# The first norm applied to the results of a projection, and its inputs loaded in pieces, in a one-core two-model kernel

## The reference

```python
def rmsnorm(x, g):
    xf = x.astype(jnp.float32)
    y = xf * lax.rsqrt(jnp.mean(xf * xf, axis=-1, keepdims=True) + EPS)
    return (y * g.astype(jnp.float32)).astype(x.dtype)

def retention_layer(h, g_norm, w_in, gn_gain, w_out):
    proj = rmsnorm(h, g_norm) @ w_in
    q, k, v, gate = jnp.split(proj, [RET_QK_W, 2 * RET_QK_W, 2 * RET_QK_W + RET_V_W], axis=-1)
    ...
    q = rotary(heads(q, RET_QK_DIM), pos)
    k = rotary(heads(k, RET_QK_DIM), pos) * (RET_QK_DIM ** -0.5)
    o = retention_chunkwise(q, k, heads(v, RET_V_DIM))
    mu = jnp.mean(o, axis=-1, keepdims=True)
    var = jnp.mean(jnp.square(o - mu), axis=-1, keepdims=True)
    o = ((o - mu) * lax.rsqrt(var + EPS)).transpose(0, 2, 1, 3).reshape(b, t, RET_V_W)
    o = o * gn_gain.astype(jnp.float32)
    y = (jax.nn.silu(gate.astype(jnp.float32)) * o).astype(h.dtype) @ w_out
    return h + y
```

## Time and profile before

| | us |
|---|---|
| median of 3 runs | 1091.26 |
| lowest and highest of them | 1089.37, 1096.87 |
| span of the profiled execution | 1088.2 |
| TensorE busy in it | 1037.3 (95%) |
| first product of unit 0 starts at | 16.92 |

### The profile page before, as it was taken

The page is one execution under the profiler, slowest core; times in us unless marked ns, Lnnn a source line. Parts: engine busy times, 40 slices in busy tenths (PEclk is TensorE's granted clock), DMA queues, the critical chain, the costliest instruction groups (busy, mean ns, idle before and its releaser), DMA issues.

```text
span 1088.2 us, 15874 instructions
## 1 busy us (share of the span) xinstructions
PE 1037.3 (95%) x6574; PEld 906.6 (83%) x6574; DVE 576.1 (53%) x708; ACT 468.7 (43%) x700; POOL 86.1 (8%) x88
## 2 busy tenths in 40 slices
PE   5999999998999999999999799997999889999996
PEld 5988778877989999977787599775788779999885
DVE  4864565456455546556535568556232455655543
ACT  5334454355554535455335545532223344444432
POOL 0000220000400001013100000002210000000000
PEclk9999999998999999999999899997798989999998
DMA  9545444543556643320254235330000235555551
GB/s 348 176 142 190 155 155 158 190 156 117 194 185 240 229 159 116 119 78 1 78 193 155 78 126 185 121 113 1 1 1 1 97 116 190 174 182 191 187 192 47
DMA packets 21555, 150.52 MB, mean 138 GB/s; under 512 B 2401, under 2 KB 2657, under 8 KB 3953
## 3 DMA queue, kind: packets, MB, share of 16 engines
q1 hardware_dynamic: 21488, 149.55, 39.5%
HBM read 148.49 MB, written 1.05 MB: 137 GB/s over the span
## 4 chain that ended last, share of the span: by engine, by line
PE 92%; DVE 3%; ACT 2%; DMA 1%; issue 1%; POOL 0%; SPq 0%; POOLq 0%; DVEq 0%
PE psum L657 90%; PE psum L991 1%; DMA ring<-in_weights 1%; ACT R L1311 1%; PE psum L731 0%; ACT xn L1311 0%; PE psum L1139 0%; ACT high_parts L1303 0%; ACT xT_parts L536 0%; PE psum L997 0%; DVE ring_parts L1631 0%; DVE h L1666 0%; ACT R L1595 0%; DVE xT_parts L546 0%; PE psum L1143 0%
## 5 line engine op out<-in xcount | busy, mean ns | idle before, releaser
L1631 DVE TENSOR_TENSOR ring_parts<-ring,high_parts 128x2048 fp32r<-128x2048 f32 x135 | 311.2, 2307 | 237.4 <-ACT high_parts L1303 236.7
L1303 ACT CAST high_parts<-ring 128x2048 fp32r<-128x2048 f32 x135 | 257.4, 1908 | 207.4 <-PE psum L657 179.1
L657 PE MATMUL psum<-xT_parts,high_parts 128*128 128x256 f32 (+1 forms) x1664 | 339.9, 283 | 1.3 <-DVE xT_parts L546 1.3
L657 PE MATMUL psum<-xT_parts,ring_parts 128*128 128x256 f32 (+1 forms) x1024 | 291.5, 285 | 0.0
L657 PEld LDWEIGHTS psum<-xT_parts,high_parts 128*128 128x128 f32 x1664 | 270.9, 189 | 1.7 <-DVE ring_parts L1631 1.5
L657 PEld LDWEIGHTS psum<-xT_parts,ring_parts 128*128 128x128 f32 x1024 | 192.8, 188 | 0.0
L657 PE MATMUL psum<-high_parts,xT_parts 128*128 128x512 f32 (+1 forms) x560 | 180.4, 399 | 1.6 <-DVE xT_parts L546 1.6
L657 PE MATMUL psum<-high_parts,R_parts 128*128 128x512 f32 (+1 forms) x560 | 167.3, 373 | 1.8 <-DVE R L2070 1.1
L657 PEld LDWEIGHTS psum<-high_parts,xT_parts 128*128 128x128 f32 (+1 forms) x560 | 103.9, 187 | 28.1 <-issue 3.2
L657 PE MATMUL psum<-ring_parts,xT_parts 128*128 128x512 f32 (+1 forms) x296 | 116.9, 395 | 0.0
L657 PEld LDWEIGHTS psum<-high_parts,R_parts 128*128 128x128 f32 (+1 forms) x560 | 99.2, 178 | 21.2 <-DVE R L2070 1.3
(11 more groups left out here) (249 smaller groups left out, 1082.7 us busy)
## 6 DMA issues: line engine op xcount, KB each, us to landing
ring<-in_weights SPq DMA_DIRECT2D x137, 1024.0 KB, 4.9
h<-in_x SPq DMA_DIRECT2D x2, 512.0 KB, 4.2
G<-in_gains SPq DMA_DIRECT2D x2, 512.0 KB, 11.8
out<-xn SPq DMA_DIRECT2D x2, 512.0 KB, 3.1
R<-in_ret_tabs SPq DMA_DIRECT2D x1, 768.0 KB, 10.1
tab<-in_tabs SPq DMA_DIRECT2D x1, 663.5 KB, 15.6
G<-in_p_t SPq DMA_DIRECT2D x1, 512.0 KB, 16.5
side_sb<-in_side SPq DMA_DIRECT2D x1, 512.0 KB, 17.2
```

The source lines that it names most:

```text
L657: return pe.matmul(out, lhsT, rhs, start=first, stop=last, skip_group_check=True)
L1303: act.copy(as_r(high[:, u % HIGH * UNIT:(u % HIGH + 1) * UNIT]), ring[:, u % RING * UNIT:(u % RING + 1) * UNIT]).then_inc(sem("units_high" ...
L1631: return dve.tensor_tensor(as_r(value), value, value_of(hi), ALU.subtract)
```

## The change

The norm of the first layer is no longer applied to `x`. TensorE turns `x` itself (`turn`), as soon as it and the identity are there. The roots come in later: spread over the partitions by two products (`spread_roots`, behind unit 2), multiplied into the rotation tables by VectorE (`token_rows`, `turned_by`), into the copies of v, into the scale of the gate's tanh (`half_rstd`) and into the roots of the group norm (`rooted`). `x` is loaded in four pieces of 128 x 512, unit 0 in four pieces of 128 x 512 issued by ScalarE's queue, and each piece is split by itself with semaphores of its own; the product of unit 0 goes piece by piece. Since unit 0 is not split by `split_units` any more, its count starts at 1.

```diff
         def split_units(engine, split, ahead):
-            done = [0]
+            done = [1]
...
-            for t in range(TT):
-                load(f"x_in{t}", hrow(t), x[t * P:(t + 1) * P, :])
+            def load_x(c):
+                for t in range(TT):
+                    load(f"x_in{t}{c}", hrow(t, c * 512, 512), x[t * P:(t + 1) * P, c * 512:(c + 1) * 512])
+
+            load_x(0)
             load("ident_in", ident, tabs[:, TB_ID:TB_ID + P])
             load("par_in", par[:, :], params)
+            load_x(1)
...
-            for u in range(2):
-                unit(u, weights[u])
+            unit(1, weights[1])
             load("ret_in", R[:, R4:R4 + NRT], ret_tabs)
...
+            def spread_roots(n):
+
+                pe.wait_ge(sem("roots"), ROOTS.index(("norm", n)) + 1)
+                bank = aux.open(pe, ("rows", n))
+                for t in range(TT):
+                    root = rstd[:, 2 * n + t:2 * n + t + 1].to_broadcast([P, P])
+                    ins = mm(bank[:, t * P:(t + 1) * P], root, ident, True, True)
+                aux.full(ins, ("rows", n), begun[0] - 2)
...
-            turn_norm("xT_ret", 0)
+            pe.wait_ge(sem("ident_in"), 16)
+            for f in range(4):
+                if f % 2 == 0:
+                    for t in range(TT):
+                        pe.wait_ge(sem(f"x_in{t}{f // 2}"), 16)
+                turn("xT_ret", f, h_tile)
             need("x", "xT_ret", 4)
-            for n in range(8):
+
+            bank = main.open(pe, ("rqk", 0))
+            w, product = next_unit(KD)
+            for f in range(4):
+                pe.wait_ge(sem(piece_low(f)), 1)
+                for half in range(2):
+                    for k in (2 * f, 2 * f + 1):
+                        ins = parts3(product, bank[:, half * T:(half + 1) * T], w(k, slice(half * P, (half + 1) * P)),
+                                     x_src(k, M, T), half == 0 and k == 0, k == KD - 1)
+            main.full(ins, ("rqk", 0))
+            for n in range(1, 8):
                 project_a([("rqk", n)], x_src, M, T)
+                if n == 2:
+                    spread_roots(0)
...
-            norm_stats(0, lambda c, t: act.wait_ge(sem(f"x_in{t}"), 16))
+            for f in range(4):
+                act.dma_start(ring[:, piece(f)], weights[0, :, piece(f)]).then_inc(sem(piece_in(f)), 16)
             act.wait_ge(sem("par_in"), 16)
+            for f in range(4):
+                high_parts("xT_ret", slice(f, f + 1))
+                act.wait_ge(sem(piece_in(f)), 16)
+                act.copy(as_r(high[:, piece(f)]), ring[:, piece(f)]).then_inc(sem(piece_high(f)), 1)
             split_up_to(1)
-            high_parts("xT_ret")
+            norm_stats(0, lambda c, t: act.wait_ge(sem(f"x_in{t}{c}"), 16))
             act.wait_ge(sem("meta_in"), 16)
...
+            act.wait_ge(sem("roots"), ROOTS.index(("norm", 0)) + 1)
...
-            dve.wait_ge(sem("ident_in"), 16)
-            norm(0)
             dve.wait_ge(sem("par_in"), 16)
+            for f in range(4):
+                low_parts("xT_ret", slice(f, f + 1))
+                dve.wait_ge(sem(piece_high(f)), 1)
+                low_part(high[:, piece(f)], ring[:, piece(f)]).then_inc(sem(piece_low(f)), 1)
...
             dve.wait_ge(sem("ret_in"), 16)
+            token_rows(0)
+            turned_by = R[:, R4 + RT_COS:R4 + RT_COS + 2 * T].rearrange("p (f t) -> p f t", f=2)
+            own.then_wait(dve.tensor_tensor(turned_by, turned_by, over(token_scale[:, M:TM], 2), ALU.mult))
...
+                rooted = rrs[:, four].rearrange("p (h t) -> p h t", t=TT)
+                own.then_wait(dve.tensor_tensor(rooted, rooted, over(rstd[:, 0:2], 2), ALU.mult))
```

More of the change, by code:

```diff
@@ L115 @@
 IS_SPLIT = [not name.startswith("ple_w_emb") for name, *_ in UNITS]
-SPLITS = [sum(IS_SPLIT[:u + 1]) for u in range(NU)]
+SPLITS = [sum(IS_SPLIT[1:u + 1]) for u in range(NU)]
 PARAM = {}
@@ L276, in aux_uses @@
 def aux_uses():
-    u = tr_uses("xT_ret", 0) + [("meta", "dve")]
+    u = tr_uses("xT_ret", 0) + [(("rows", 0), "dve"), ("meta", "dve")]
     u += [(("rs", h), "dve") for h in range(RH)]
@@ L427, in two_models_kernel @@
         power = cols(1)
+        half_rstd = cols(8)
         msum = cols(3)
@@ L525, in two_models_kernel @@
         turned("xT_ffn", range(4), (into_x, gain_of("ffn_norm_w_2")))
[L527 to L552, removed]
+        def turned_high(act, name, wait, some=slice(None)):
+            for key, parts, frees in [turn for turn in turns if turn[0][0] == name][some]:
+                bank = wait(aux, key)
+                if name == "xT_kv" and frees:
+                    act.wait_ge(sem("kv_low"), key[1] + 1)
+                for n, (kt, (hi, _), g) in enumerate(parts):
+                    ins = act.activation(as_r(hi), bank[:, n * T:(n + 1) * T], ACT.Copy, scale=g)
+                ins.then_inc(sem("turned_high"), 1)
@@ new lines, in turned_low @@
+        def turned_low(dve, name, wait, some=slice(None)):
+            for n_turn, (key, parts, frees) in [(n, turn) for n, turn in enumerate(turns) if turn[0][0] == name][some]:
+                bank = wait(aux, key)
+                dve.wait_ge(sem("turned_high"), n_turn + 1)
+                for n, (kt, (hi, lo), g) in enumerate(parts):
+                    ins = dve.scalar_tensor_tensor(as_r(lo), bank[:, n * T:(n + 1) * T], g, value_of(hi),
+                                                   ALU.mult,
+                                                   ALU.subtract)
+                if frees:
+                    aux.free(ins, key)
+                else:
+                    ins.then_inc(sem("kv_low"), 1)
@@ L1320, in norm_stats, with high_parts, gate_tanh @@
                         square(n, c, t, h, trash)
-            def high_parts(name):
-                turned_high(act, name, wait)
+            def high_parts(name, some=slice(None)):
+                turned_high(act, name, wait, some)
             gates = [0]
-            def gate_tanh(key, before):
+            def gate_tanh(key, before, scale=0.5):
                 i = gates[0]
@@ L1348, in _ @@
                     bank = wait(main, key)
-                    main.free(act.copy(R[:, R2 + t * 2048 + c * 512:R2 + t * 2048 + (c + 1) * 512], bank), key)
+                    main.free(act.activation(R[:, R2 + t * 2048 + c * 512:R2 + t * 2048 + (c + 1) * 512], bank, ACT.Copy,
+                                             scale=rstd[:, t:t + 1]), key)
             act.wait_ge(sem("rotated"), 8)
@@ L1639, in _, with low_parts @@
             wait, after_read, split_up_to = split_units(dve, split_low, HIGH - 1)
-            def low_parts(name):
-                turned_low(dve, name, wait)
+            def low_parts(name, some=slice(None)):
+                turned_low(dve, name, wait, some)
             def roots(n):
@@ L1660, in norm, with token_rows @@
                 to_diagonal(n)
+            def token_rows(n):
+                bank = wait(aux, ("rows", n))
+                aux.free(dve.tensor_copy(token_scale[:, M:TM], bank[:, 0:T]), ("rows", n))
+                after_read(aux, ("rows", n))
             def add_to_h(keys):
```

43 lines of the change are left out of this document (33 added, 10 removed).

## The result

| | before | after |
|---|---|---|
| median of 20 runs each, us | 1096.7 | 1103.89 |
| lowest and highest, us | 1088.77, 1101.53 | 1098.63, 1110.4 |
| span of the profiled execution, us | 1088.2 | 1108.6 |

What follows compares the result with a forecast made beforehand. TensorE, busy 95% of the span, was taken to bound the kernel. Start and clock in unit 0 3.65, roots' products 0.45 and wait at unit 4 2.1 sum to 6.2 us slower: 1091.26 to 1097.5, range 1092 to 1101.5.

Steps and rivals of the forecast that it cites:

- unit 1 lands: Opening: unit 1's transfer lands at 11.75 us as before, since the same bytes stand ahead of it.
- first product: Start of unit 0 on TensorE: at about 18.75 us instead of 16.92, behind unit 1's cast, table load and VectorE's pieces.
- lower clock in unit 0: Unit 0: TensorE, idle before, runs its first 4.0 us at the lower clock; the unit takes 7.5 us, not 5.68.
- roots' products: Behind unit 2: two added float32 products of 128 columns on TensorE cost +0.45 us.
- wait for units 2, 3: Units 2 and 3: their rests, later behind the meta tokens, stay hidden behind TensorE's work; term 0.
- wait at unit 4: Start of unit 4: TensorE waits for VectorE's copy, multiplication, two rotations and rest of unit 4; +2.1 us.
- units 4 to 7 behind it: After the wait at unit 4: VectorE's later work hides and units take 5.68 us each as before; no term.
- unit 1 lands earlier: Rival, opening: unit 1 lands about 2.4 us earlier since its queue no longer carries unit 0; +3.8 us in all, chance 0.06.
- the rival of the upper clock: Rival, unit 0: TensorE already at the upper clock, +4.2 us in all; chance 0.16, shared with a free table load.
- the clock's fall behind it: Rival, unit 4: the new wait lowers the clock for 4 us, costing 1.9; +8.1 us in all, chance 0.14.
- The change does what its words say: Rival, opening: unit 0's first quarter comes first, TensorE starts near 10 us; -0.6 us, held excluded by the order.
- Not slower, by other lower-clock stretches: Rival, 717 to 890 us: three or four fewer lower-clock stretches of 1.9 us each offset the loss; chance 0.07.

Runs made afterwards that it cites:

- e5: Changed kernel with 30 filler products of 128 columns on TensorE in the pause before unit 0; 1100.91 us (one run).
- e1: Changed kernel with turned banks of x numbered -2, so unit 0's quarters are split before unit 1; 1097.65 us, ratio to before 1.0022.
- e3: Changed kernel with a one-column copy on ScalarE ahead of the wait for unit 1, so the table load runs beside the transfers; 1102.6 us (one run).
- e11: Changed kernel with unit 0 loaded in one transfer, still on ScalarE's queue, x still in four pieces; 1101.83 us (one run).
- e10: Changed kernel with x loaded in two transfers as before, unit 0 still in quarters on ScalarE's queue; 1097.48 us (one run).
- e2: Changed kernel with VectorE splitting up to unit 4 before it waits for the roots' rows; 1102.22 us, ratio to before 1.0109 (four runs).
- e4: Changed kernel with the transfers of before: x in two, unit 0 in one, all on SyncE's queue; 1108.96 us (one run).
- e7: Changed kernel with unit 0's four quarters issued by SyncE's queue instead of ScalarE's; 1110.91 us (one run).
- e6: Changed kernel with the edits of e1, e2 and e3, and unit 2 split ahead of the meta tokens; 1093.8 us, ratio to before 0.9972.
- e12: e6 with the transfers of before (x in two, unit 0 in one, all on SyncE's queue); 1093.47 us, ratio to before 0.9974.

## Why the prediction was right or wrong

The sign was right and so was "within 1%"; the predicted 1097.5 and the range to 1101.5 were not, with a median of 1103.89.

**The step that failed first is the base.** "The median of the runs, 3.1 us above that span, from 1091.26": three runs of a kernel whose 20 executions lie in clusters over 12.8 us don't fix a median, and all 20 gave 1096.7. The prediction says that the runs spread by 7.5 us and still allows "about 2 us for the medians' own spread". With the 6.2 on the base of 20 runs the time would have been 1102.9, 1 us off. That nearness is partly luck: the median of before was 3 us lower in two of its three later sets, and the 6.2 themselves were too small, 3.2 short of what the trace shows at M.

**The sum, against the 9.4 of the trace:**

| step | predicted | measured | |
|---|---|---|---|
| unit 1 lands | 11.75 | 13.12 | too early by 1.37 |
| first product | 18.75 | 20.22 | that, and 0.10 |
| lower clock in unit 0 | +1.82 (7.5 - 5.68) | +1.86 (e5) | right |
| roots' products | +0.45 | 0.36 | right |
| wait for units 2, 3 | none | none | right |
| wait at unit 4 | 2.1 | 2.08 | right |
| units 4 to 7 behind it | as before | 24.50 against 22.99 (e5) | too low by 1.5 |

Unit 4 was forecast at 18.75 + 7.5 + 2 x 5.68 + 0.45 + 5.68 + 2.1 = 45.84 and came at 47.60, 1.76 late; M was forecast at 68.93 and came 3.17 late, so 1.41 arose behind unit 4.

*The start.* The order gave the path correctly: cast of unit 1 first, the load on the path with 1.28 and no drain, VectorE pacing the pieces. e1 and e3 moved the first product by 7.1 and 1.3 us as that path says. What failed is that I kept the old landing because "the engines of both queues move the same bytes". They do, but in pieces: unit 0 in quarters held the landing back by 1.5 us (e11) and the two more pieces of `x` by 0.6 (e10). The rival "unit 1 lands earlier" was wrong in sign.

*The clock.* The reading of counts over the printed column was right, and the rival of the upper clock is refuted by e5. (Its price has a slip: 48 products of 0.118 us from 18.75 on end at 24.4, not at 24.3, so it comes to +4.4 instead of +4.2.) *The wait at unit 4* was right in place and size, and e2 shows that it is made by the rest of unit 4 standing behind the two rotations. But I gave the clock's fall behind it 0.14. It fell in the kernel after, e1, e3, e4, e7 and e10, and not in e5 and e11: 6 of 8 profiles with this wait, at 1.5 us each, somewhat less than the 1.9 assumed. A rival with a row on either side, at 1.8 and at 2.51 us, deserved about half, and taken into the sum at 1.5 us it would have made 7.7.

*"The change does what its words say"*, -0.6, was excluded by the order, rightly. Its price was not right: e1 gives +2.6. I took the meta tokens at their old landing of 19.79, and with the new transfers they land at 21.2 and hold unit 2; the clock's fall comes on top.

*"Not slower, by other lower-clock stretches"* was the right mechanism in a wrong role. It is real, larger than thought (10.3 us between two profiles), and the runs of one kernel differ in their mean granted clock (0.954 to 0.968 over the 20 of after). It belongs to the base and its spread, not to what the change does.

## What to carry to other kernels

Where waits split work "up to n ahead", read the built order of each engine before costing an edit: here one count that started at -1 put a whole unit and a table load ahead of the small pieces that were meant to come first, and reordering one split took out a wait and the slower clock behind it. Splitting a transfer has a price of its own, in issues and in what is queued behind it: here it did not pay with the consumer far back in line (after), nor with the consumer next in line (e6 against e12). And before a forecast of a fraction of a per cent, ask how many runs stand behind the base, and compare traces at a mark behind the change, not by their spans.

## What the runs showed of the hardware that I had not expected

- The granted clock prints 1.00 at the start of unit 0 while products step by 0.22 us instead of 0.118. In e11 the column shows 0.50 in the same place, with 6 products:

```profile
20.20:21.20 1.00, 1.00 (x6) 0.50 1.06 422
```

- A pause of 2.1 us was followed by a lower clock in 6 profiles and not in 2, at the same place of nearly the same program.
- Four transfers of 256 KB in place of one of 1 MB delayed the next 1 MB by 1.5 us: between 2 and 4 us the DMA engines were busier (0.90 against 0.75 in e11) and moved less (215 GB/s against 260).
- One program's executions fall into clusters over some 12 us, and their mean granted clock goes with them: of the 20 of after, the fastest (1098.63) had 0.968, the six near 1101 had 0.962 or 0.963, the five near 1110 had 0.954.
